# Two heads' value products side by side, and ScalarE's and VectorE's order of work around the norms of a two-layer trunk

## The reference, cut to what matters

```python
def rms_norm(x, g):
    y = x * lax.rsqrt(jnp.mean(x * x, axis=-1, keepdims=True) + 1e-6)
    return y * g

for i in range(2):
    h = h + 0.5 * rms_norm(swiglu(rms_norm(h, g[0]), w_gu, w_down), g[1])
    hn = rms_norm(h, g[2])
    m = rwkv7_time_mix(hn, ...) if i == 0 else swa_attention(hn, ...)
    h = h + rms_norm(m, g[3])
    h = h + 0.5 * rms_norm(swiglu(rms_norm(h, g[4]), w_gu, w_down), g[5])

# attention, per chunk of 64 queries; keys: the 16 meta tokens, the chunk before, the chunk
lc = einsum('bcqgrd,bckgd->bgrcqk', qc, kb) * 64 ** -0.5 + bias
pc = softmax_with_sink(lc, sink)
oc = einsum('bgrcqk,bckgd->bcqgrd', pc, vb)
```

## Time and profile before

| | us |
|---|---|
| median of 3 runs (lowest, highest) | 2269.2 (2268.21, 2269.91) |
| profiled execution | 2274.56 |
| its span, first to last instruction | 2272.7 |
| TensorE busy | 2187.8 (96%) |
| VectorE busy | 1087.5 (48%) |
| ScalarE busy | 803.5 (35%) |
| GpSimd busy | 466.4 (21%) |
| mean granted TensorE clock | 0.973 |

### The profile page before, as it was taken

How to read it: one execution, slowest core, us unless ns; L and a number is a source line. 1 busy time by engine, 2 the same in 40 slices (tenths; PEclk the granted TensorE clock), 3 DMA queues, 4 the chain that set the end, 5 groups by cost and what they waited for, 6 DMA issues and landing times.

```text
span 2272.7 us, 50953 instructions
## 1 busy us (share of the span) xinstructions
PE 2187.8 (96%) x22780; PEld 1865.3 (82%) x22780; DVE 1087.5 (48%) x1546; ACT 803.5 (35%) x1389; POOL 466.4 (21%) x597
## 2 busy tenths in 40 slices
PE   7999998999899989999999999999998999999997
PEld 6888887877699967788888888888886667888886
DVE  5433324867565666743332553432374627433323
ACT  5333313565233353433332343332142324433320
POOL 2111112430223324411110321110151204111102
PEclk9999999999999999999999999999998769999999
DMA  4323321310000022233332132233132012323311
GB/s 160 131 93 103 125 89 38 132 68 19 13 4 4 4 76 78 80 129 105 115 122 80 46 112 94 93 127 116 38 112 65 1 37 75 112 95 118 128 52 38
DMA packets 29099, 183.43 MB, mean 81 GB/s; under 512 B 3232, under 2 KB 8160, under 8 KB 9936
## 3 DMA queue, kind: packets, MB, share of 16 engines
q1 hardware_dynamic: 28032, 178.79, 22.4%
q0 software_dynamic: 848, 1.37, 0.3%
HBM read 174.31 MB, written 4.30 MB: 79 GB/s over the span
## 4 chain that ended last, share of the span: by engine, by line
PE 84%; DVE 11%; ACT 3%; issue 1%; POOL 1%; DMA 0%; SPq 0%; POOLq 0%; DVEq 0%; ACTq 0%
PE psum L289 67%; PE psum L1642 6%; DVE arena L355 2%; DVE arena L403 1%; PE psum L1633 1%; PE psum L381 1%; PE psum L2519 1%; PE psum L2518 1%; PE psum L2505 1%; PE psum L1666 1%; DVE arena L393 1%; DVE arena L331 1%; DVE split L264 1%; PE psum L2349 1%; DVE h L360 1%
## 5 line engine op out<-in xcount | busy, mean ns | idle before, releaser
L289 PE MATMUL psum<-x,split 128*128 128x256 f16 (+1 forms) x5568 | 637.6, 276 | 7.7 <-POOL x L422 6.1
L289 PEld LDWEIGHTS psum<-x,split 128*128 128x128 f16 x5568 | 543.5, 98 | 97.5 <-issue 13.6
L289 PE MATMUL psum<-x,arena 128*128 128x256 f16 (+2 forms) x2448 | 282.5, 276 | 8.1 <-DVE arena L657 6.8
L289 PE MATMUL psum<-x,split_more 128*128 128x256 f16 (+1 forms) x2496 | 288.0, 276 | 2.5 <-DVE x L2617 1.5
L725 POOL TENSOR_TENSOR arena<-arena 128x256 f16<-128x256 f32 (+1 forms) x176 | 120.1, 682 | 798.9 <-ACT arena L574 798.9
L289 PEld LDWEIGHTS psum<-x,split_more 128*128 128x128 f16 x2496 | 244.9, 98 | 40.1 <-issue 1.9
L289 PEld LDWEIGHTS psum<-x,arena 128*128 128x128 f16 (+1 forms) x2448 | 240.8, 99 | 44.2 <-DVE arena L264 7.3
L264 DVE SCALAR_TENSOR_TENSOR split<-stage,split 128x2048 f16<-128x2048 f32 (+1 forms) x77 | 189.9, 2466 | 157.5 <-ACT split L258 157.5
L289 PE MATMUL psum<-arena,split 128*128 128x256 f16 (+1 forms) x2304 | 261.0, 275 | 0.0
L289 PEld LDWEIGHTS psum<-arena,split 128*128 128x128 f16 x2304 | 225.2, 98 | 34.7 <-issue 2.5
L652 DVE SCALAR_TENSOR_TENSOR arena<-psum,arena 128x256 f32<-128x256 f32 (+1 forms) x176 | 75.6, 429 | 311.0 <-ACT arena L568 306.5
(11 more groups left out here) (218 smaller groups left out, 2575.8 us busy)
## 6 DMA issues: line engine op xcount, KB each, us to landing
stage<-in_w_gu SPq DMA_DIRECT2D x88, 1024.0 KB, 4.9
stage<-in_w_down SPq DMA_DIRECT2D x32, 1408.0 KB, 6.1
stage<-in_w_rkv SPq DMA_DIRECT2D x12, 1024.0 KB, 4.9
stage<-in_w_out SPq DMA_DIRECT2D x4, 1024.0 KB, 5.1
stage<-in_w_q SPq DMA_DIRECT2D x4, 1024.0 KB, 4.8
stage<-in_w_o SPq DMA_DIRECT2D x4, 1024.0 KB, 6.0
h_spill<-h SPq DMA_DIRECT2D x1, 2112.0 KB, 11.9
out<-h SPq DMA_DIRECT2D x8, 256.0 KB, 2.1
```

The source lines that it names most:

```text
L289: last = pe.matmul(o, wt(wp, k), xs(xp, k), start=(k == 0 and wp == 0 and xp == 0), stop=(k == tiles - 1 and wp == 1))
```

## The change

Five edits. In `values`, the two band products of a key head come first, then its two meta products. At the start of the FFN after a mixer, ScalarE takes the first sigmoid (`gate(0, 0)`) ahead of all squares of h and `high(0, 0)` ahead of the last four; in the other turns that order stays. VectorE takes the first gated product there right after the inverse, ahead of the scaling, puts the split of the fourth up weight between the scaling of tiles 4 and 5, and the second gated product behind the scaling. TensorE's `pre_total` there moves from product 1 of part 0 of the fourth up step to the beginning of part 1. At the end of the first three FFNs ScalarE squares all eight tiles of h in one go, ahead of the square of out tile 5 and of the split of the second weight.

```diff
@@ -344,12 +344,14 @@
             e.wait_ge(h_new[s], BY_POOL * (T.post + 1))
             e.wait_ge(h_own[s], BY_DVE * (T.post + 1))
 
-        def post_scale(dve, T, s):
+        def post_scale(dve, T, s, between=None):
             a, n = T.spans[s]
             dve.wait_ge(post_dve[s], T.post + 1)
             if T.x_before[s]:
                 dve.wait_ge(x_lo[1 - s], BY_POOL * T.x_before[s])
             for k in range(KT):
+                if between and k == BY_POOL:
+                    between()
                 if k >= 4:
                     h_ready(dve, T, s, k - 4)
                 dve.scalar_tensor_tensor(out=tmp[:, k % 4, 0:n], in0=mix_out[:, k, a:a + n],
@@ -539,7 +541,7 @@
                     up(e, 0, 0, None if late else ((0, 6), post_total))
                     up(e, 1, 0, ((0, 1), post_total) if late else None)
                     up(e, 2, 0, None if late else ((0, 4), pre_total))
-                up(e, 3, 0, ((0, 1), pre_total) if not opening and late else None)
+                up(e, 3, 0, ((1, 0), pre_total) if not opening and late else None)
                 for m in range(4):
                     up(e, m, 1)
                 for m in range(4, FT):
@@ -591,10 +593,16 @@
                 else:
                     post_root(e, T, 1)
                     split_hi(e, ups[3])
-                    square_h(e, T, 1, 0, 4)
-                    gate(0, 0)
-                    square_h(e, T, 1, 4, KT)
-                    high(0, 0)
+                    if T.after_mixer:
+                        gate(0, 0)
+                        square_h(e, T, 1, 0, 4)
+                        high(0, 0)
+                        square_h(e, T, 1, 4, KT)
+                    else:
+                        square_h(e, T, 1, 0, 4)
+                        gate(0, 0)
+                        square_h(e, T, 1, 4, KT)
+                        high(0, 0)
                     gate(1, 0)
                     warm(e, ACT.Sqrt)
                     pre_root(e, T, 1)
@@ -633,10 +641,9 @@
                         squares(m, 1)
                     post_root(e, T_out, 1)
                     return
-                square_h(e, T_out, 0, 0, 5)
+                square_h(e, T_out, 0)
                 squares(5, 1)
                 split_hi(e, T_out.jobs[1])
-                square_h(e, T_out, 0, 5, KT)
                 pre_root(e, T_out, 0)
                 T_out.how.high(e, T_out, 0)
                 squares(6, 1)
@@ -668,6 +675,13 @@
                     split_lo(e, ups[3])
                     T.how.scale(e, T, 1)
                     gated(1, 0)
+                elif T.after_mixer:
+                    post_inverse(e, T, 1)
+                    gated(0, 0)
+                    post_scale(e, T, 1, lambda: split_lo(e, ups[3]))
+                    gated(1, 0)
+                    pre_inverse(e, T, 1)
+                    T.how.scale(e, T, 1)
                 else:
                     post_inverse(e, T, 1)
                     post_scale(e, T, 1)
@@ -2512,11 +2526,14 @@
                     e.wait_ge(t_dve2.sem, t_dve2.count("tm1", i))
                     e.wait_ge(a_pool.sem, a_pool.count("v", i))
                     after(e, o_dve2, "lo", i - 1)
-                    for u in range(8):
-                        g, par = u // 2, u % 2
-                        o_ = psum[par * HD:(par + 1) * HD, 7, g * P:(g + 1) * P]
-                        e.matmul(o_, vx[0:nb, s, g * HD:(g + 1) * HD], ptb[0:nb, u], start=True, stop=False)
-                        last = e.matmul(o_, v_meta[:, g * HD:(g + 1) * HD], ptm[:, u], start=False, stop=True)
+                    for g in range(KV):
+                        outs = [psum[par * HD:(par + 1) * HD, 7, g * P:(g + 1) * P] for par in range(2)]
+                        for par in range(2):
+                            e.matmul(outs[par], vx[0:nb, s, g * HD:(g + 1) * HD], ptb[0:nb, 2 * g + par],
+                                     start=True, stop=False)
+                        for par in range(2):
+                            last = e.matmul(outs[par], v_meta[:, g * HD:(g + 1) * HD], ptm[:, 2 * g + par],
+                                            start=False, stop=True)
                     last.then_inc(o_pe.sem, o_pe.step("o"))
 
                 scores(0)
```

## The result

| | before | after |
|---|---|---|
| median of four runs each, us | 2268.7 | 2248.0 |
| lowest and highest | 2267.48, 2269.91 | 2246.61, 2252.31 |
| profiled execution | 2274.56 | 2247.17 |
| its span | 2272.7 | 2245.3 |
| mean granted TensorE clock | 0.973 | 0.982 |

The ratio is 0.9904 (95% interval 0.9890 to 0.9919): 20.7 us faster, where 23.1 were forecast. The profiled executions differ by 27.4 us, more than the medians, since that of before took 5.9 us more than the median of its runs and that of after 0.8 less.

A forecast was written before the change was run, and what follows sets the result against it. TensorE was taken to bound the kernel, with 84% of the chain. Pairs 15.5, turns after the two mixers 5.7 and FFN-end squares 1.9 sum to 23.1 us, off the median 2269.2 giving 2246.1; range 2241 to 2258.

The forecast's parts named there:

- The pairs: Attention's values steps: two band, then two meta products; the second of two alike costs 0.11 us at full clock; saves 15.5.
- the turns: FFN start after both mixers: reordered work shrinks TensorE's waits and the total over squares; 3.4 and 2.3, together 5.7 us.
- the step of 8.12 us: Second-last values step at attention's end: about 6.7 products at 0.36 and 9.3 at 0.61, falling to 4.6, saving 3.5.
- first chunk: First values step in attention, all at half clock: saves 3.2 us, under its chunk's cap of 3.8.
- the next four: Four attention chunks, 1764.94 to 1813.11: save 3.6 us, the cap set by VectorE and ScalarE, lasting 44.6.
- the fifth: Fifth attention chunk after the first values step: from 13.10 us to 11.1, saving 2.0.
- the end: Attention from 1826.21 to 1850.19, where TensorE sets everything: its last two values steps save 3.5 and 3.2 us.
- one after the other: Rival, chance 0.20: in value pairs only the emptying goes, the second product costs 0.24 us; 16.6 saved, 2252.6.
- nothing saved in a pair: Rival, chance 0.12: in values the second load waits for the first product's end, as now; 7.6 saved, 2261.6.
- Slower: Rival, chance 0.04: granted clock stays at 0.50 through all attention chunks and pairs save nothing; +10.9, 2280.1 us.
- the turns give nothing: Rival, chance 0.06: after the mixers late squares leave the totals ending where they do now, pairs overlap; 15.5 saved, 2253.7.
- The squares at the FFN ends: Ends of the first three FFNs: squares no longer wait for the second split; 1.7, 0.1 and 0.1, together 1.9 us.

The follow-up runs named there:

- the doubled bands: The kernel before with each band product of the values step done twice in a row into the same place; its one execution took 2269.9 us.

## Why the prediction was right, and what was off

The range held the time. The pairs carried it, and their mechanism is shown; that their size came out as well is partly luck, and the turns were mis-sized. By terms:

**The pairs, forecast 15.5: 16.1 measured alone.** Right in size, but by errors that cancel. The second of a pair was to cost 0.11 us; it costs none, since both start together. I had read the 0.11 off the corners in the earlier trace rows as the step from one product to the next, when it is half the step of two that start together. With the true price the prediction's own chain gives 3.8+3.6+2.0+4.1+5.0 = 18.5, since only the middle chunks are capped by the loop of VectorE and ScalarE. There was a slip besides: the step of 8.12 us, with half its products at the lower prices, comes to 5.4 by the forecast's own numbers (4.8 if the clock falls at the same moment as before) and not 4.6.

Against the forecasts: first chunk 4.0 (3.2, with a cap named at 3.8), the next four 3.4 (3.6; they last 44.75 for 44.6), the fifth 2.2 (2.0), the end 9.75 (6.7). The end is off because its last values step, forecast at 9.95-3.2 = 6.7 us of half clock, took 3.52 at 0.81. These are differences of two profiles and sum to 19.3; 16.1 was timed. The stretch around attention, from ScalarE's root of h ahead of it (about 1676) to its first root behind it (about 1878), took 202.2 us in both profiles of before, but 199.0 and 199.3 with the same code in those of the turns and the squares alone, and 181.9 to 184.2 in the five profiles with the new order of values and the old one of ScalarE (that with added work left out). So the profile of before had some 3 us in it that most runs probably lack, and from 199 the new order gains 15 to 17, in line with the 16.1 timed. With 2.9 behind the first mixer, of which more below, that comes near the 5.9 by which this profile stood above its median. The prediction read a saving too small off a stretch too long, and the two cancel.

Of the rivals, *one after the other* (0.24) and *nothing saved in a pair* are ruled out by the starts at 1780.13. *Slower* is ruled out too: the granted clock over the four chunks rose from 0.79 to 0.89 though TensorE idles a quarter of the time.

The Trainium skill (TensorEngine Tiling, Key Properties) says that a change of the tiling mode drains TensorE and that different tiles work in parallel; the traces agree with both: a repeat with the same rows costs 0.22 us, a product with a change of rows 0.36, so the emptying is about 0.15, and two column halves overlap wholly. The Trainium skill (TensorE: Matmul & The Clock Gate, Part 3) lets a weight load overlap with matmuls only where the row group differs; here the row group was the same, and the four weight loads of a pair ran from 1780.13 to 1780.33, beside products of the pair that began at 1780.13 and lasted to 1780.57. The measurement decides against that rule as stated. The prediction's word that every load starts only when its predecessor is nearly done was wrong within a product even before: both loads of the product at 1794.04 had ended by 1794.23, while its first instruction ran to 1794.36.

**The turns after the two mixers, forecast 5.7: 1.4 measured alone (by the interval from 3.2 faster to 0.9 slower), and 0.4 of the wrong sign in the whole.** This is the term that was mis-sized, and its rival, *the turns give nothing*, fits the time; but not for the reason I gave it. The steps came nearly as written: waits of 0.38 and 1.06 for the fourth step (forecast at most 0.3 and about 0.6; both splits took 2.81, with a GpSimd addition beside them, in place of 2.29), totals of 3.62 begun on time, new waits of 1.50 and 1.66 (forecast 1.6), the last square at 1896.1 with its total not held up.

What failed first is the other side of the subtraction, "the total ends at 942.3 in place of 945.7 since it then takes 3.5 in place of 6.2". The 6.2 was not a property of the old order. The same code behind the same 3.1 us took 6.24, 6.27 and 6.23 us in three executions, 4.65 in one, and 3.62 in three (the squares alone, the doubled bands, the change without turns). Of the 3.4 of the first mixer 2.6 therefore were the clock of the execution I read; where the old order ran at full clock it loses only 0.3 to the new one.

At the second mixer the old order is slower in every profile (the total takes 4.7 to 6.0 for 3.62), and with the wait the change brings the root behind it 1.7 to 2.0 us earlier than five of those profiles and 3.0 earlier than two. But some 0.6 is lost behind it in four of the five profiles with the moved total: there TensorE waits for x, and the granted clock over the following 9 us is 0.82. This is the window behind the total after:

```profile
1898.56:1907.56 9.00, 6.80 (x44) 4.10 (x43) 8.07 (x12) 4.95 (x11) 4.69 (x6) 0.82 0.00 1
```

With the 0.3 at the first mixer that leaves 0.3+1.2 = 1.5 by the profiles with the higher clock, close to the 1.4 timed, whose interval is wide. That 0.6 the forecast had put at nothing. And it did not weigh the place of the total against the old one: moved so that it would not be held up, it gives away the 2.3 us found above. Why the clock falls behind the first mixer in some executions and not in others stays open.

**The squares at the FFN ends, forecast 1.9: 2.1 measured alone (by the interval from 3.6 faster to 0.2 slower).** The mechanism came as written, with VectorE's split as the cover that it named: against the profile of before 1.8 at the first FFN (forecast 1.7), and 0.3 each at the second and third (forecast 0.1). But the 1.7 has the same flaw as the turns. The last six instructions of the total behind their wait of 3.1 us took 3.09 us at a granted 0.50 in the execution I read. In the six profiles with the old order they took 3.09 (three times), 2.74, 1.91 and 1.64, and VectorE's wait ahead of the inverse, which is what the change can take away, was 1.7, 1.34, 0.52 and 0.25. TensorE's and VectorE's timelines with the least of it, from the kernel before with the high part first:

```profile
378.00 1.64 PE L381 MATMUL psum<-arena,cst 128*128 128x272 f32 x6 [3.10 <-ACT arena L375]
```
```profile
380.21 1.85 DVE L393 RECIPROCAL arena<-arena 128x272 f32<-128x272 f32 x1 [0.25 <-ACT arena L387]
```

So the first FFN gives between 0.3 and 1.8 us, by the clock that an execution gets.

**The sum.** 23.1 was 15.5+5.7+1.9; measured alone 16.1+1.4+2.1 = 19.6, as a whole 20.7. Two of three terms came out within 0.6, one of them by errors that cancel; the excess is the turns'. Taking the gain off the median with the words "waits and work, not drift" was wrong for all three in part: in the profile read, some 3 us of attention, 2.6 of the first mixer and up to 1.4 of the first FFN were just that drift. For the pairs the low saving made up for it. Among the rivals, *the turns give nothing* should have kept the 1.9 of the squares: 2251.8 and not 2253.7.

## What to carry to other kernels

Small products that alternate between numbers of rows pay for the emptying each time, so put those with the same rows and different columns next to each other: the second is free here. When TensorE's need falls below that of the next loop, read that loop's own order at once; an edit worth nothing before (the high part ahead of the exponentials) was then worth 10 us, half of what the whole change had given. And before a stretch at a lowered clock is counted as a gain, read it in a second profile of the same kernel: here 2.6 us of a gain of 5.7 were missing in three of seven executions, and most of one of 1.7 in two of six.

## What the runs showed of the hardware

- Two f32 products of 128x128 onto the two column halves, on the same 128 rows, start together and take 0.37 us with the change of rows behind them, the same as one (0.36); at a granted 0.50 the pair takes 0.62.
- A product more in the same tile costs 0.22 us at 1.00 and 0.42 at half clock (a triple of 1.65 for 1.23, in the first step, whose band products have 64 rows), and the change between 128 and 16 rows 0.15 more at 1.00.
- Half as many products again made the values steps only 4.1 us longer in sum (65.23 for 61.10), and the one execution no slower. The profile calls TensorE busy throughout in both, and both change the number of rows 16 times a step; yet that of before ran at 0.65 and 0.50 of 2.4 GHz late in attention, and the denser one at 1.00. Whether other executions do the same was not tried.
- The same 16 f32 instructions behind the same wait of 3.1 us took 3.62 us at 1.00 in three executions, 4.65 in one and 6.2 in three others, at 0.58 in the one of the earlier trace rows; six such instructions at the end of the first FFN took 1.64 at 1.00 in one and 3.09 at 0.50 in another.
